# Two mixer stages' ends in a three-layer transformer kernel: y loads moved ahead of a weight tile, sums and low rows moved sooner, output pieces split around the turns and PV

## The reference, cut to what matters

```python
for i in range(DEPTH):            # i = 0: MLA, i = 1: SWA
    h = rmsnorm(x, layer_norm[i])
    y, gate = mixer(h, ...)       # attention; y is 512 x 2048
    x = x + (y * jax.nn.silu(gate)) @ w_out
```

## Time and profile before

| | us |
|---|---|
| median of 3 runs | 2104.36 (2100.88 to 2104.91) |
| the profiled execution, its own time | 2101.91 |
| its span | 2100.1 |
| TensorE busy | 2085.3 (99%) |
| VectorE, ScalarE, GpSimd busy | 1412.1, 995.4, 190.5 |

### The profile page before, as it was taken

The page is one execution under the profiler, slowest core; times in us unless marked ns, Lnnn a source line. Parts: engine busy times, 40 slices in busy tenths (PEclk is TensorE's granted clock), DMA queues, the critical chain, the costliest instruction groups (busy, mean ns, idle before and its releaser), DMA issues. The chain is left out here.

```text
span 2100.1 us, 29980 instructions
## 1 busy us (share of the span) xinstructions
PE 2085.3 (99%) x9730; PEld 1737.2 (83%) x9730; DVE 1412.1 (67%) x2574; ACT 995.4 (47%) x1928; POOL 190.5 (9%) x197
## 2 busy tenths in 40 slices
PE   9999999999999999999999999999999999999999
PEld 7888888888888888888887788888888888888887
DVE  6677777777733568888888633777777677769432
ACT  6444444445422446666666633544454445446221
POOL 0111111112101000000000122200000000003000
PEclk9999999999999999999999999999999999999999
DMA  7324444445633624444444733633434233435742
GB/s 225 102 70 114 111 112 113 114 112 171 211 82 98 195 64 123 125 127 127 127 127 121 256 100 100 185 89 93 116 92 134 74 111 107 109 109 155 218 112 70
DMA packets 404542, 262.56 MB, mean 125 GB/s; under 512 B 18689, under 2 KB 377345, under 8 KB 404481
## 3 DMA queue, kind: packets, MB, share of 16 engines
q1 hardware_dynamic: 395744, 254.03, 42.8%
q10 hardware_dynamic: 8736, 7.74, 1.5%
HBM read 210.33 MB, written 24.12 MB: 112 GB/s over the span
## 5 line engine op out<-in xcount | busy, mean ns | idle before, releaser
L638 PE MATMUL pp<-act_hi,w_hi 128*128 128x512 f32 x2304 | 903.7, 392 | 5.7 <-DVE w_lo L612 2.9
L640 PE MATMUL pp<-act_hi,w_lo 128*128 128x512 f32 x2304 | 898.1, 390 | 0.0
L639 PE MATMUL pp<-act_lo,w_hi 128*128 128x512 f32 x2304 | 897.8, 390 | 0.0
L612 DVE TENSOR_TENSOR w_lo<-raw,w_hi 128x512 fp32r<-128x512 f32 x680 | 455.7, 702 | 361.1 <-ACT w_hi L604 360.3
L604 ACT ACTIVATE w_hi<-raw 128x512 fp32r<-128x512 f32 (+1 forms) x684 | 395.9, 622 | 456.6 <-PE pp L640 230.1
L638 PEld LDWEIGHTS pp<-act_hi,w_hi 128*128 128x128 f32 x2304 | 433.1, 188 | 98.8 <-DVE w_lo L612 5.8
L640 PEld LDWEIGHTS pp<-act_hi,w_lo 128*128 128x128 f32 x2304 | 432.8, 188 | 91.1
L639 PEld LDWEIGHTS pp<-act_lo,w_hi 128*128 128x128 f32 x2304 | 433.3, 188 | 87.1 <-issue 0.2
L657 POOL TENSOR_TENSOR pT_lo<-gathered,pT_hi 128x640 fp32r<-128x640 f32 x30 | 46.5, 1570 | 358.7 <-ACT pT_hi L653 358.7
L1314 ACT ACTIVATE prob<-ps,minus,q_scale 128x512 f32<-128x512 f32 (+1 forms) x64 | 39.0, 615 | 78.3 <-DVE minus L1394 78.3
L638 PE MATMUL ps<-act_hi,w_hi 128*128 128x512 f32 x176 | 69.4, 394 | 0.0
(11 more groups left out here) (432 smaller groups left out, 2756.6 us busy)
## 6 DMA issues: line engine op xcount, KB each, us to landing
raw<-w_in SPq DMA_DIRECT2D x48, 1024.0 KB, 5.9
raw<-swa_w_in SPq DMA_DIRECT2D x36, 1024.0 KB, 5.8
raw<-mla_w_in SPq DMA_DIRECT2D x23, 1024.0 KB, 5.8
raw<-mla_w_out SPq DMA_DIRECT2D x16, 1024.0 KB, 6.4
raw<-swa_w_out SPq DMA_DIRECT2D x16, 1024.0 KB, 6.0
raw<-w_out SPq DMA_DIRECT2D x16, 1024.0 KB, 6.5
gathered<-turned SPq DMA_DIRECT2D x224, 56.0 KB, 2.0
x_feature_major<-xT SPq DMA_DIRECT2D x8, 1024.0 KB, 9.6
```

Source lines behind the costliest of these rows:

```text
L612: q.eng.tensor_tensor(dst, raw_piece(tile, p), high, ALU.subtract).then_inc(s_lo, tile.ups(p))
L638: q.eng.matmul(psum[:, :], wh, ah, start=start and n == 0, stop=False)
L639: q.eng.matmul(psum[:, :], wh, al, start=False, stop=False)
L640: last = q.eng.matmul(psum[:, :], wl, ah, start=False, stop=stop and n == PIECE // P - 1)
```

## The change

In words. `STEPS`: two new ScalarE steps `end_low0`, `end_low1` ahead of `norm1`. SP, for SWA alone: `load_y` of parts 0 and 1 ahead of weight tile 1 of the output; part 2 stays behind the store. MLA's last unit: output piece 2 ahead of `turn(3)` (it was behind), two chunks of piece 3 between `turn(3)` and `turn(2)`, the other two behind `turn(0)`. SWA's unit 16: one chunk of piece 5 behind `pv()`, not two, and behind it three chunks each of pieces 6 and 7; `output_T` of layer 2 then does chunk 3 of each alone. SWA's unit 15: on ScalarE both weight pieces 0 and 1 and the copies of the low rows come ahead of `normalise(1)`; on VectorE the former pair's sums come ahead of `this_lo(2)`, and `this_lo(3)` goes behind the subtractions of the turned blocks. In unit 16 `first_lo(1)` goes ahead of `inverse(1)`. The arithmetic is the same.

```diff
@@ attention_dmas
             load_tile(q.eng, Tile(f"out{n}", 0, 0))
             if phase == "mla":
                 gather(units - 1)
+            else:
+                load_y(q, n, 0)
+                load_y(q, n, 1)
             load_tile(q.eng, Tile(f"out{n}", 0, 1))
             if phase == "swa":
                 store_y(q, phase, units - 1, units - 3, "V.y_prev")
-            for part in range(3):
+            for part in range(0 if phase == "mla" else 2, 3):
                 load_y(q, n, part)
             store_y(q, phase, units - 1, units - 2)
@@ mla_T
+            if not proj:
+                early_output(q, 1, 2, 3)
             turn(3, None)
             if attn:
                 gate_piece(2)
             if not proj:
-                early_output(q, 1, 2, 3)
+                early_output(q, 1, 3, 4, range(0, 2))
             turn(2, None)
             turn(1, "V.pt_lo3")
             turn(0, None)
             if not proj:
-                early_output(q, 1, 3, 5)
+                early_output(q, 1, 3, 4, range(2, 4))
+                early_output(q, 1, 4, 5)
@@ output_T
-                early_output(q, n, EARLY, 2 * PIECES)
+                early_output(q, n, EARLY, 2 * PIECES, range(3 if n == 2 else 0, PIECE // P))
                 unit(1)
@@ swa_T
                 turn(1)
-                early_output(q, 2, 5, 6, range(0, 2))
+                early_output(q, 2, 5, 6, range(0, 3))
                 pv()
-                early_output(q, 2, 5, 6, range(2, 4))
+                early_output(q, 2, 5, 6, range(3, 4))
+                early_output(q, 2, 6, 8, range(0, 3))
                 return
@@ swa_A, low_prev
-                    q.eng.activation(...).then_inc(*q.did(f"low_prev{half}"))
+                    q.eng.activation(...).then_inc(*q.did(f"{'end_low' if ends else 'low_prev'}{half}"))
@@ swa_A
             this_hi(0)
+            if ends:
+                this_hi(1)
+                low_prev(0)
+                low_prev(1)
             normalise(1)
-            this_hi(1)
+            if not ends:
+                this_hi(1)
             if attn:
                 q.eng.wait_ge(*q.at("V.gate"))
                 q.eng.activation(s_th[:, :], s_gate, ACT.Tanh, scale=0.5).then_inc(*q.did("tanh"))
             this_hi(2)
-            low_prev(0)
-            low_prev(1)
+            if not ends:
+                low_prev(0)
+                low_prev(1)
             this_hi(3)
@@ swa_V, sum_prev
-                q.eng.wait_ge(*q.at(f"A.low_prev{half}"))
+                q.eng.wait_ge(*q.at(f"A.{'end_low' if ends else 'low_prev'}{half}"))
@@ swa_V
+            first_lo(1)
             inverse(1)
-            first_lo(1)
@@ swa_V
-            this_lo(2)
             if ends:
                 sum_prev(0)
                 sum_prev(1)
+            this_lo(2)
@@ swa_V
-            this_lo(3)
+            if not ends:
+                this_lo(3)
```

More of the change, by code:

```diff
@@ L141 @@
         "T": "s00 s01 s10 s11 pv_prev0 pv_prev1 t00 t01 t10 t11 pv0 pv1".split(),
-        "A": ("exp00 exp01 exp02 exp03 sink0 exp10 exp11 exp12 exp13 sink1 norm0 norm1 tanh low_prev0 low_prev1 q_hi0 q_hi1 "
+        "A": ("exp00 exp01 exp02 exp03 sink0 exp10 exp11 exp12 exp13 sink1 norm0 end_low0 end_low1 norm1 tanh low_prev0 low_prev1 q_hi0 q_hi1 "
               "turned_hi pt_hi00 pt_hi01 pt_hi10 pt_hi11 y_low0 y_low1").split(),
@@ L2068, in low_prev @@
                     q.eng.wait_ge(*q.at(f"T.pv_prev{half}"))
-                    q.eng.activation(s_y_low[0:HD2, half, :], PAIR_BANK[half][HD2:P, :], ACT.Copy).then_inc(*q.did(f"low_prev{half}"))
+                    q.eng.activation(s_y_low[0:HD2, half, :], PAIR_BANK[half][HD2:P, :], ACT.Copy).then_inc(*q.did(f"{'end_low' if ends else 'low_prev'}{half}"))
             def gathered_hi():
```

## The result

The changed kernel takes 2106.55 us (median of 20 runs, 2105.43 to 2107.75) against 2103.6 of the kernel before (20 runs): ratio 1.0015, 95% interval 1.0009 to 1.0021, some 3 us slower. The profiled execution's span grew from 2100.1 to 2103.6 us. Sums of the distances from one matmul's start to the next, less the plain distance for its size, place the growth: -1.4 us in the first 50 us of the run, where the two kernels are the same (in the traces of the experiments this stretch is 1.8 us shorter to 1.3 us longer than before, so this part isn't the change's), +0.5 at the MLA end, +4.2 between 1100 and 1200 us, where SWA ends, and 0.2 elsewhere.

The account below looks back on a forecast made before the run. TensorE was taken as the bound, busy 99%, with 7.0 us of gaps to win. MLA +0.6 and SWA -0.8 summed to -0.2 us: 2101.7 for the profiled execution, 2104.2 for the median, range 2099.0 to 2107.4.

Parts of the forecast that it names:

- +0.6 at MLA: MLA end: two old gaps (1.3 us) go, a new wait and restart (1.8 + 0.1) come; bounds -1.3 to +1.1.
- -0.8 at SWA: SWA end, units 15 and 16 together: -0.8 us, with bounds of -4.3 and +2.5.
- 4.2 us as the least: Whole kernel: a difference below 0.2% of 2104 us, 4.2 us, can't be told from no change.
- 1.8 us at piece 4: MLA end: TensorE newly waits 1.8 us at output piece 4 for VectorE's act_lo of chunk 8.
- Unit 15: SWA unit 15: gap before turn(0) goes, 0.45 us wait before PV replaces 1.17; PV starts 2.1 us sooner.
- What the moved load costs: SWA unit 15: later tile delays the y_prev store to 1160.45, y to 1160.55; 2.1 us spent, and 0.45 more.
- three steps of 0.6 us later: VectorE after unit 15's y: next_lo(2), next_lo(3), then y_lo(0) at 1162.4; TensorE's first output piece at 1163.2.
- forecast gap of 3.7 us: TensorE at SWA unit 16's first output piece, waiting for VectorE: the prediction's listed sign was a gap over 3 us.
- Unit 16 and the last gap: SWA unit 16: first_lo(1) earlier turns +0.45 into -0.5; wait before PV 0.9; gap and restart of 0.57 before chunk 15 gone.
- The early store: Rival, SWA unit 15: y_prev store lands before 1156.7 without following the tile; -4.3 us, 2100.7 with MLA loss; chance 0.22.
- The collision: Rival, SWA end: second y load still running delays tile and store; by 2 us 2106.2, beyond that 2108.6; chance 0.10.

Follow-up runs that it names:

- experiment 9: Changed kernel with store of y_prev ahead of weight tile 1, and at MLA's end y_hi of chunks 8-11 and y_lo of 8-9 ahead of block work: 2096.01 us.
- experiment 1: Changed kernel with one edit: SP issues the store of y_prev ahead of output weight tile 1 instead of behind it; 2097.66 us, ratio 0.9974 to the kernel before.
- experiment 2: Changed kernel, SP's order kept, but y of SWA unit 15 written to a buffer of its own, so without waiting for the y_prev store; 2097.44 us, ratio 0.9972.
- experiment 3: Changed kernel with this_lo(3) back ahead of the turned blocks' subtractions in SWA unit 15, SP's order as changed; 2103.55 us, ratio 1.0003 to the kernel before.
- experiment 7: Changed kernel with the store of y_prev ahead of weight tile 1 but all y loads behind the tile; 2104.39 us, ratio 1.0005 to the kernel before.
- experiment 5: Changed kernel with the MLA end as before: output piece 2 behind turn(3), pieces 3 and 4 behind turn(0); 2105.58 us, ratio 1.0012 to the kernel before.
- experiment 4: Changed kernel where, in SWA unit 16, GpSimd's subtractions of chunks 4 to 7 wait until VectorE reaches the maxima; 2104.06 us, ratio 1.0004 to the kernel before.
- experiment 6: Kernel before with SP's edit alone: y loads 0 and 1 ahead of weight tile 1, store of y_prev behind it; 2104.43 us, ratio 1.0004.

## Why the prediction was wrong

It said 2104.2 us, 0.2 below the median that it had for the kernel before, from +0.6 at MLA and -0.8 at SWA. It came out 3 us slower than before. That the time itself, 2106.55, is only 2.4 us from the forecast is in part luck: with 20 runs the kernel before has a median of 2103.6, not 2104.36. These runs also tell 3 us from nothing, where the prediction took 4.2 us as the least.

**MLA, +0.6: right.** A wait of "1.8 us at piece 4" was foretold, 1.64 plus a restart of about 0.1 came; the end as a whole is 0.5 us longer. Its cause, the order behind the later turn, is shown by experiment 9, which moves the splits of chunks 8 and 9 ahead on ScalarE and VectorE together; it doesn't part the two engines.

**Unit 15: right.** No gap before `turn(0)`; the `pT_lo` subtractions sooner by 1.9 us after allowing for 0.6 us by which this trace is ahead (2.1 said); a wait before PV of 0.64 where 0.45 was said.

**"What the moved load costs": right in its mechanism.** The tile waits for the moved split, the store stands behind the tile, `y` behind the store: 1160.86 against the 1160.55 said, or 0.9 later with the 0.6 us allowed for. Experiments 1 and 2 show it from two sides. That was the first term to be too small: the store took 7.1 us, not 6.1. The second y load, issued at 1148.08, landed 7.3 us later and so was in flight when the tile and the store were issued; that it is the reason is likely from experiments 3 and 7, but the runs that keep this order vary by themselves (6.7 in experiment 2, 7.2 in experiment 5).

**The step that failed is the next one, "three steps of 0.6 us later", which put TensorE's first piece at 1163.2.** It started at 1165.64, or 1166.26 with the 0.6 us allowed for. Of the three steps two took 0.6 us and the third, the second weight subtraction, 1.68; the y subtraction behind them took 1.74 and not 0.69. That is 2.1 us, and it comes of GpSimd, which now subtracts at the same time: experiment 4 gives these steps their 0.6 back by moving GpSimd alone. The prediction asked what frees VectorE and never what the early y loads start on GpSimd. The rows of before have GpSimd starting only behind VectorE's y subtractions of 1161.92, and VectorE already slow beside GpSimd's eight subtractions at the MLA end:

```profile
528.62 1.76 DVE L612 TENSOR_TENSOR w_lo<-raw,w_hi 128x512 fp32r<-128x512 f32 x1
...
1165.23 5.30 POOL L1544 TENSOR_TENSOR act_lo<-y_whole,act_hi 128x512 fp32r<-128x512 f32 x4 [21.19 <-ACT act_hi L1534]
```

**The same term goes on behind the first piece.** From that piece to unit 16's first turn the forecast had 11.6 us; it took 13.5 (1165.64 to 1179.10). VectorE needed 5.0 us from the end of its first y subtraction to the end of the weight subtraction that TensorE's second piece waits for, where experiment 1 has 3.0.

**A cost left out: the granted clock.** The forecast gap of 3.7 us was itself long, and no cost was put on what follows a gap. The first 12 matmuls behind the gap took 5.3 us (1165.64 to 1170.93) where 12 at full clock take 2.7. But the thirteenth could not start before VectorE's weight subtraction ended at 1170.46, so of these 2.6 us the clock cost at most 0.5, an estimate from these rows; the rest is VectorE's. In experiment 4 it cost nothing more, in experiment 3 about 1 us by the second piece. The Trainium skill ("TensorE: Matmul & The Clock Gate", section "Why this matters for your kernels") warns that idle gaps between bursts of matmuls bring the clock down to half; the traces agree as far as every gap of 4.4 us and more did so, and single gaps of up to 1.6 before the change did not. They also show a fall without a long gap, behind the three of 1.0 to 1.2 us in experiment 6. The forecast, with a gap of 3.7 of its own, should have priced the rival that this rule makes.

Together: 0.9 for the store, 2.1 for the shared stretch with GpSimd up to the first piece, and 1.8 behind it (the same stretch, with at most 0.5 for the clock) make 4.8 of the 5.0 us between -0.8 and the +4.2 that the trace has.

**Unit 16 and the last gap.** `first_lo(1)` ahead of `inverse(1)` took away the 0.90 gap (experiment 1, where TensorE isn't late, has none there either), the split the last one; the wait before the second PV rose to 0.9 from start to start, as said.

**The rivals.** The early store, priced at -4.3 us at SWA and 2100.7 with the MLA loss, is what experiment 1 built: -4.5 at the SWA end, so rightly priced; its 2097.7 is lower still, as the kernel before has 2103.5 on that chip and not 2104.36 and the first 50 us of the trace are 1.3 us shorter; some 0.6 us stay open. The prediction had no row of a store alone; experiment 7 has one, 2.0 us against its estimate of 2.6, which went by a fit for DMAs that GpSimd issues, while SP issues this one. The collision, given 0.10, was partly real: 1 us in the changed kernel, where the y load in flight is the likely reason, and 2.6 in experiment 3. In all seven traces in which the store was issued behind the tile it landed behind it.

## What to carry to other kernels

When an instruction is moved later, follow every transfer whose issue it permits, then every transfer queued behind that one, and ask whose buffer waits for those: here a 0.6 us subtraction moved by 2 us held a store that nothing seemed to need, and 9 us hung on one line's place. A transfer made earlier also wakes engines earlier; look at what they will then run beside. Price a long gap on TensorE (here 4 us and more) with the slow matmuls behind it, and then ask whether the next piece would have waited for another engine anyway: here most of the slow matmuls' time was covered so.

## What the runs showed of the hardware

- VectorE and GpSimd subtracting at once, both with two operands in SBUF: VectorE's 128x512 float32 subtraction takes up to 1.75 us instead of 0.68 (2.36 and 3.42 for two, 1.28 with GpSimd held back), GpSimd's four take 6.83 instead of 5.30. The multiply at L2196, with one operand in PSUM, took 0.68 right between them, as ever. The Trainium skill ("GPSIMD Engine Reference", section "1. Specifications") has the two sharing their SBUF interfaces, with contention where VectorE reads two SBUF inputs; both sides of that agree here.
- A store of 256 KB lands 2.0 us after its issue with no y load and no tile ahead of it on SP's queue (experiment 7), and 5.7, 6.1, 7.1 or 8.7 us after it, according to what was issued in the few us before it on the same queue. No run shows a store that overtook the tile ahead of it.
- Behind gaps of 4.4 to 6.7 us without a matmul the first matmuls run at a granted clock of 0.50: until about 1170.1 in the changed kernel, 1169.7 in experiment 4, 1172.3 in experiment 3. In experiment 6 the clock fell to 0.50 behind three gaps of 1.0 to 1.2 us. The busy time of the page doesn't show it, only the clock of a narrow window and the distance of the starts do.
